# Attention inside a two-part transformer kernel: value products turned round, weights normalised on GpSimd before they are turned

## What is computed

```python
proj = u @ w_in
o_a = dsa_attention(aq, ak, av, iq, ik, iw)      # 4 heads, one shared key and value, the best 64 keys of each query
o_b = moba_attention(bq, bk, bv)                 # 4 heads, causal here (256 tokens are one block)
o_c = forgetting_attention(cq, ck, cv, log_f)    # 8 heads, score + cumsum(log_f)[query] - cumsum(log_f)[key]
o_c = o_c * jax.nn.sigmoid(cg)                   # a gate for each of the 512 output columns of o_c
return jnp.concatenate([o_a, o_b, o_c], axis=-1) @ w_out
```

## Time and profile before

| | |
|---|---|
| median of 3 runs | 2230.54 us (2229.44 to 2232.28) |
| the profiled execution | 2230.91 us, span 2229.2 us |
| PE busy | 2142.9 us, 96% of the span |
| DVE, ACT, POOL busy | 47%, 34%, 3% |
| attention turns of the first layer | 1438.9 to 1473.2 us in the span |
| attention turns of the second layer | 1973.8 to 2011.2 us in the span |

### The profile page before, as it was taken

One profiled execution on the slowest core, in us unless ns is written; L12 is line 12 of the kernel. 1 busy time (PEld: TensorE's weight loads), 2 busy tenths in 40 slices (PEclk: granted clock), 3 DMA queues, 4 the chain that ended last, 5 costly groups with the idle time before them and its releaser, 6 DMA issues.

```text
span 2229.2 us, 27344 instructions
## 1 busy us (share of the span) xinstructions
PE 2142.9 (96%) x10940; PEld 1422.5 (64%) x10940; DVE 1051.4 (47%) x1559; ACT 764.8 (34%) x1099; POOL 72.5 (3%) x100
## 2 busy tenths in 40 slices
PE   8999999988999999999889999999999999999999
PEld 6663333333486333333348888878888888888887
DVE  5830000001383000000147777768777777866776
ACT  4732111110272111111033436654335435565332
POOL 3000000000000000000100002000000000300000
PEclk9999999999999999999999999999999999999999
DMA  8389999999949999999985555235565554415551
GB/s 290 151 358 428 428 428 427 427 427 426 387 184 388 427 427 428 428 428 428 426 313 191 172 185 173 93 116 189 189 199 177 171 194 159 153 58 180 187 197 59
DMA packets 169816, 618.29 MB, mean 277 GB/s; under 512 B 7816, under 2 KB 116528, under 8 KB 145904
## 3 DMA queue, kind: packets, MB, share of 16 engines
q1 hardware_dynamic: 167248, 612.00, 70.8%
q0 software_dynamic: 2464, 4.84, 0.8%
HBM read 615.76 MB, written 1.05 MB: 277 GB/s over the span
## 4 chain that ended last, share of the span: by engine, by line
PE 76%; DMA 13%; DVE 4%; ACT 4%; SPq 1%; DVEq 1%; issue 1%; ACTq 0%
PE W L2172 20%; PE W L2419 12%; PE W L2420 6%; DMA moe_own<-in_moe_w 5%; DMA moe_split<-in_moe_w 4%; PE acc L2023 4%; PE acc L2027 4%; PE acc L2024 4%; PE W L1995 3%; PE W L1997 3%; PE W L1996 3%; PE W L2154 2%; DMA moe_raw<-in_moe_w 2%; DMA moe_xt<-in_moe_w 2%; PE W L2423 2%; PE acc L2163 2%
## 5 line engine op out<-in xcount | busy, mean ns | idle before, releaser
L1267 DVE TENSOR_TENSOR w_lo<-raw,w_hi 128x2048 fp32r<-128x2048 f32 (+2 forms) x203 | 445.0, 2195 | 168.9 <-ACT w_hi L771 160.4
L771 ACT ACTIVATE w_hi<-raw 128x2048 fp32r<-128x2048 f32 (+2 forms) x203 | 372.2, 1833 | 305.5 <-PE acc L2027 134.5
L2419 PE MATMUL W<-xT_both,w_hi 128*128 128x512 f32 x1218 | 438.1, 399 | 4.2 <-DVE xT_both L1285 3.4
L1543 DVE TENSOR_TENSOR hid<-W,hid 128x512 f32<-128x512 f32 x32 | 22.1, 691 | 732.2 <-PE W L2172 732.2
L2420 PE MATMUL W<-xT_both,w_lo 128*128 128x256 f32 x1218 | 341.7, 281 | 0.0
L2419 PEld LDWEIGHTS W<-xT_both,w_hi 128*128 128x128 f32 x1218 | 229.2, 188 | 55.4 <-issue 4.0
L2420 PEld LDWEIGHTS W<-xT_both,w_lo 128*128 128x128 f32 x1218 | 230.1, 189 | 7.0
L2172 PE MATMUL W<-moe_split,xe 128*64 128x512 f32 x672 | 150.5, 595 | 9.1 <-DMA moe_split<-in_moe_w 9.1
L2172 PE MATMUL W<-moe_own,xe 128*64 128x512 f32 x608 | 137.3, 596 | 12.5 <-DMA moe_own<-in_moe_w 12.4
L1995 PE MATMUL W<-w_hi,xT_both 128*128 128x474 f32 (+1 forms) x376 | 145.4, 387 | 0.0
L1996 PE MATMUL W<-w_lo,xT_both 128*128 128x474 f32 (+1 forms) x376 | 142.7, 380 | 0.0
(11 more groups left out here) (409 smaller groups left out, 2944.4 us busy)
## 6 DMA issues: line engine op xcount, KB each, us to landing
moe_split<-in_moe_w SPq DMA_DIRECT2D x60, 2048.0 KB, 29.9
moe_raw<-in_moe_w SPq DMA_DIRECT2D x54, 2048.0 KB, 31.8
moe_own<-in_moe_w SPq DMA_DIRECT2D x54, 2048.0 KB, 29.5
raw<-in_ffn_w_gate SPq DMA_DIRECT2D x44, 1024.0 KB, 5.1
raw<-in_ffn_w_up SPq DMA_DIRECT2D x44, 1024.0 KB, 5.1
raw<-in_ffn_w_down SPq DMA_DIRECT2D x44, 1024.0 KB, 4.8
moe_xt<-in_moe_w SPq DMA_DIRECT2D x18, 2048.0 KB, 34.0
raw<-in_w_in SPq DMA_DIRECT2D x32, 948.0 KB, 4.8
```

What stands on the lines that cost most here:

```text
L771: s.activation(part(w_hi[split_slot(c)], cols), part(raw[slot_of(c)], cols), ACT.Copy).then_inc(hi_ready, 1)
L1267: v.tensor_tensor(part(w_lo[split_slot(c)], cols), part(raw[slot_of(c)], cols), part(w_hi[split_slot(c)], cols).bitcast(F32), ALU.subtract ...
L2419: t.matmul(wide, hi[:, cols], xT_both[:, kc].rearrange("p h t -> p (h t)"), start=(kc == 0), stop=False)
```

## The change

- `finish` goes. DVE takes the reciprocal of the row sums right after the exponentials (`reciprocal_sums`), POOL multiplies the weights in place by it, four instructions a unit, and PE waits for POOL (`normal`) instead of ACT (`p`) before it turns the weights.
- The value product takes the 64 value columns of a head as the stationary matrix and streams 128 turned weights; two heads go to the two halves of the PSUM partitions. The result is already [head columns, tokens], so `turn_result` and `attn` go.
- The gates are turned once, after `decays`, and DVE copies them to `gate_T`. `apply_gate` multiplies the result in PSUM; `upper_result` on ACT and `lower_result` on DVE write the two halves that the output product reads.
- The forget sums of eight heads are packed into one product (four instructions for sixteen, a copy of 256 columns for 1024); `head_rows`, made by POOL, picks a head's row.
- `split` and `rest` of one chunk of `w_out` (c + 18) move from ahead of the first exponentials to behind unit 0's copy on ACT and behind `chosen_bias(0)` on DVE.

PE still waits for `at` of unit u-2 at the head of turn u. The semaphore is now raised by `lower_result`. The core of the diff:

```diff
@@ POOL, ahead of the turns and in them
                 g.memset(nlf_wide[:], 0.0)
+                g.tensor_tensor(head_rows[:], ident[:, 0:C_HEADS // 2].unsqueeze(2).to_broadcast([P, C_HEADS // 2, P]),
+                                ident[:, HD:HD + C_HEADS // 2].unsqueeze(2).to_broadcast([P, C_HEADS // 2, P]), ALU.add)
...
+                for u in range(8):
+                    n = P * (UNITS[u][0] + 1)
+                    pool.wait_ge(mx["recip"], 8 * l + u + 1)
+                    for i in range(4):
+                        last = g.tensor_scalar(Sb[:, u % 2, i, 0:n], Sb[:, u % 2, i, 0:n], asum[:, u, i:i + 1], None, ALU.mult)
+                    last.then_inc(mx["normal"], 1)
@@ ACT
-                split(c + 18, D)
...
+                def upper_result(u):
+                    b, grp = UNITS[u]
+                    if grp >= 2:
+                        act.wait_ge(mx["gated"], 4 * l + u - 1)
+                    else:
+                        act.wait_ge(mx["o"], (lay.times(8) + (u + 1)).v)
+                    s.activation(xT_hi[:, 2 * grp:2 * grp + 2, b * P:(b + 1) * P],
+                                 acc[:, 2 + u % 2, 0:SEQ].rearrange("p (a t) -> p a t", a=2), ACT.Copy).then_inc(mx["hi"], 1)
...
-                s.activation(decay_rows[:], acc[:, 0:2, :].rearrange("p a (i k) -> p (a i) k", k=SEQ), ACT.Copy).then_inc(mx["decay_sb"], 1)
+                s.activation(decay_rows[:], acc[:, 0, 0:SEQ], ACT.Copy).then_inc(mx["decay_sb"], 1)
                 for u in range(8):
...
-                    if u == 6:
-                        attention_halves(range(3))
+                    if u == 0:
+                        split(c + 18, D)
+                    else:
+                        upper_result(u - 1)
+                upper_result(7)
@@ DVE
+                def reciprocal_sums(u):
+                    dve.wait_ge(mx["p"], (lay.times(8) + (u + 1)).v)
+                    v.reciprocal(asum[:, u, :], asum[:, u, :]).then_inc(mx["recip"], 1)
+                def apply_gate(u):
                     b, grp = UNITS[u]
                     dve.wait_ge(mx["o"], (lay.times(8) + (u + 1)).v)
...
+                    v.tensor_tensor(result(u), result(u), gate_T[:, 2 * (grp - 2):2 * (grp - 1), b * P:(b + 1) * P], ALU.mult)
+                    v.drain().then_inc(mx["gated"], 1)
+                def lower_result(u):
+                    b, grp = UNITS[u]
+                    dve.wait_ge(mx["hi"], (lay.times(8) + (u + 1)).v)
+                    own = (slice(None), slice(2 * grp, 2 * grp + 2), slice(b * P, (b + 1) * P))
+                    v.tensor_tensor(xT_lo[own], result(u), xT_hi[own].bitcast(F32), ALU.subtract).then_inc(mx["at"], 1)
...
-                rest(c + 18, D)
                 maxima(0)
                 maxima(1)
+                dve.wait_ge(mx["gates"], l + 1)
+                v.tensor_copy(gate_T[:].rearrange("p k t -> p (k t)"), acc[:, 2:4, :].rearrange("p a n -> p (a n)"))
+                v.drain().then_inc(mx["gate_sb"], 1)
+                reciprocal_sums(0)
                 for u in range(8):
                     if u == 0:
                         best_keys(0, 4, 8)
                         chosen_bias(0)
+                        rest(c + 18, D)
                     elif u < 5:
                         best_keys(1, 2 * (u - 1), 2 * u)
                         if u == 4:
                             chosen_bias(1)
+                    if u < 7:
+                        reciprocal_sums(u + 1)
                     if u + 2 < 8:
                         maxima(u + 2)
...
-                    finish(u)
+                    if UNITS[u][1] >= 2:
+                        apply_gate(u)
+                    if u > 0:
+                        lower_result(u - 1)
+                lower_result(7)
@@ PE
+                    t.matmul(acc[:, 0, 0:SEQ], nlf_wide[:, 0, :], tri[:], start=True, stop=False)
+                    t.matmul(acc[:, 0, P:SEQ], nlf_wide[:, 1, :], tri[:, 0:P], start=False, stop=True).then_inc(mx["decay"], 1)
+                def turn_gates():
+                    for k in range(4):
+                        for b in range(TB):
+                            last = t.transpose(acc[:, 2 + k // 2, SEQ * (k % 2) + b * P:SEQ * (k % 2) + (b + 1) * P],
+                                               proj[:, b, CG + P * k:CG + P * (k + 1)], ident[:])
+                    last.then_inc(mx["gates"], 1)
...
+                turn_gates()
                 for u in range(8):
                     b, grp = UNITS[u]
                     if u == 0:
                         pe.wait_ge(mx["decay_sb"], l + 1)
+                        pe.wait_ge(mx["gate_sb"], l + 1)
                     if u >= 2:
 
                         pe.wait_ge(mx["at"], (lay.times(8) + (u - 1)).v)
                     if u < 6:
                         keep_warm(4, u)
-                    pe.wait_ge(mx["p"], (lay.times(8) + (u + 1)).v)
+                    pe.wait_ge(mx["normal"], (lay.times(8) + (u + 1)).v)
...
-                    if u == 6:
+                    if u == 7:
                         pe.wait_ge(mx["at"], (lay.times(8) + 6).v)
-                        pe.wait_ge(mx["p"], (lay.times(8) + 8).v)
-                        for q in TURN_ORDER[:3]:
-                            turn_result(q)
...
                     pe.wait_ge(mx["te"], (lay.times(8) + (u + 1)).v)
...
+                    for pair in range(2):
                         for kb in range(b + 1):
+                            for r in range(2):
+                                h = 2 * pair + r
+                                hh = 4 * (grp - 2) + h
+                                col = (AV, BV + HD * h, CV + HD * hh, CV + HD * hh)[grp]
+                                last = t.matmul(acc[HD * r:HD * (r + 1), 2 + u % 2, P * pair:P * (pair + 1)], proj[:, kb, col:col + HD],
+                                                PT[:, 2 * r + pair, kb * P:(kb + 1) * P], start=(kb == 0), stop=(kb == b))
                     last.then_inc(mx["o"], 1)
```

More of the change, by code:

```diff
@@ L325, in build_program @@
         place[0] = after_qkt
-        attn = at("attn", [P, TB, D])
+        gate_T = at("gate_T", [P, 4, SEQ])
         Sb = at("Sb", [P, 2, 4, SEQ])
@@ L348, in build_program @@
         score2 = in_proj("score2", 1, AQ, [P, SEQ])
-        decay_rows = in_proj("decay_rows", 0, CQ, [P, C_HEADS // 2, SEQ])
-        nlf_wide = in_proj("nlf_wide", 1, CQ, [P, TB, C_HEADS // 2, P])
+        decay_rows = in_proj("decay_rows", 0, CQ, [P, SEQ])
+        head_rows = in_proj("head_rows", 0, CQ + SEQ, [P, C_HEADS // 2, P])
+        nlf_wide = in_proj("nlf_wide", 1, CQ, [P, TB, P])
         acc = ctx.enter_context(nc.psum_tensor("acc", [P, 4, 512], F32))
@@ L1809, in chosen_bias, with result @@
                     v.drain().then_inc(mx["bias"], 1)
-                def finish(u):
+                def result(u):
+                    return acc[:, 2 + u % 2, 0:SEQ].rearrange("p (a t) -> p a t", a=2)
+                def reciprocal_sums(u):
+                    dve.wait_ge(mx["p"], (lay.times(8) + (u + 1)).v)
+                    v.reciprocal(asum[:, u, :], asum[:, u, :]).then_inc(mx["recip"], 1)
+                def apply_gate(u):
                     b, grp = UNITS[u]
                     dve.wait_ge(mx["o"], (lay.times(8) + (u + 1)).v)
[L1815 to L1826, removed]
+                    v.tensor_tensor(result(u), result(u), gate_T[:, 2 * (grp - 2):2 * (grp - 1), b * P:(b + 1) * P], ALU.mult)
[5 more added lines that the diff above has]
+                    v.tensor_tensor(xT_lo[own], result(u), xT_hi[own].bitcast(F32), ALU.subtract).then_inc(mx["at"], 1)
                 def maxima(u):
@@ L1914, in mixer @@
                             chosen_bias(1)
+                    if u < 7:
+                        reciprocal_sums(u + 1)
                     if u + 2 < 8:
                         maxima(u + 2)
-                    if u == 6:
-                        attention_rests(range(3))
-                    if u == 7:
-                        rest(c0 + (C_MIX_OUT + AHEAD), D)
-                    finish(u)
-                attention_rests((3,))
-                for k in range(1, KC - 2):
+                    if UNITS[u][1] >= 2:
[3 more added lines that the diff above has]
+                lower_result(7)
+                for k in range(0, KC - 2):
                     rest(c0 + (C_MIX_OUT + k + AHEAD), D if k + AHEAD < KC else SLOT)
@@ L2597, in scores @@
                             half = slice(HD * (h % 2), HD * (h % 2 + 1))
-                            t.matmul(W[:, k, o:o + n], tri[half, P:2 * P], decay_rows[half, hh // 2, 0:n], start=False, stop=False,
+                            t.matmul(W[:, k, o:o + n], head_rows[half, hh // 2, :], decay_rows[half, 0:n], start=False, stop=False,
                                      skip_group_check=True)
@@ L2633, in mixer @@
                         scores(u + 2)
[L2634 removed]
+                    if u == 7:
```

(5 more changed lines are left out.)

47 lines of the change are left out of this document (4 added, 43 removed).

## The result

The kernel after takes 2256.35 us (2254.43 to 2257.01), the one before 2230.39: a ratio of 1.0113 (95% interval 1.0101 to 1.0125), 26 us slower where 9.3 were forecast and 2252 was the top of the range. The profiled execution took 2257.01 us with a span of 2255.1. The whole difference lies in the two attention stretches: from the first scores to the first idle product behind the output chunks the first layer takes 77.69 us (1433.79 to 1511.48) where it took 64.02 (1433.44 to 1497.46), the second 79.12 where it took 67.25. That is 25.5 of the 26.

What follows compares the result with a forecast made beforehand. PE was taken as close to the bound, DVE behind it. Profiled execution 2230.91 + 6.1 for two layers' walk + 3.1 for the clock gave 2240.1, the median 0.4 lower at 2239.7 us; range 2230 to 2252.

Steps and rivals of the forecast that it cites:

- The mechanism forecast: Attention turns: PE waits for `at`, now raised behind maxima and gate on DVE; with about one more clock fall, chance 0.42.
- a wait of PE that ends on POOL: Sign in the profile after that would show the forecast wrong: PE's wait ending on POOL; no size given.
- The sum: Whole kernel: profiled execution 2230.91 + 6.1 for two layers + 3.1 for the clock = 2240.1 us, median 2239.7.
- so I take the first: POOL's multiplication ahead of the turnings, priced as one-input: 4 x 0.39 us for 256 keys, 4 x 0.29 for 128.
- the count of the clock's falls: Attention stretches: one fall of PE's clock in both layers instead of in one, +3.1 us.
- saves nothing there: Unit 2 to 3: PE idles about 2 us after the value product, so its shortening gains nothing; interval +1.8 us.
- The nearer wait: Head of PE's turn: `at` of unit u-2 comes one DVE turn later; unit 2 to 3 takes 6.05 instead of 4.27 us.
- POOL is the bound: Rival: POOL's multiplications at 0.953 us, four taking 3.8, add 6 us a layer: 2248.6 us; chance 0.08.
- those on the clock: Rivals: lower clock no oftener or never, 2236.6 or 2233.5 us, chance 0.27; low through most turns, 2245 to 2258, 0.10.
- the loop: Scores, maxima, gate and rest must follow one another before PE's next turn: 6.05 us from unit 2 to 3.
- Edits costed at nothing: `head_rows` on POOL, moved `split` and `rest`, ACT's short copies and POOL's queued loads: claimed hidden under waits or slack, 0 us.
- the late reciprocal: Unit 0 to 1: unit 1's reciprocal queues on DVE behind key search, mask and moved `rest`; interval +2.3 us.

Runs made afterwards that it cites:

- the mended kernel: After with POOL in one instruction, lower_result first, unit 1's reciprocal inside the key search, split and rest in units 5 and 6, some warming products: 2227.42 us.

## Why the prediction was right in direction and wrong in size

The mechanism forecast, PE held by `at` through DVE's queue, is in the trace, but it is not alone: PE also waits 5.7 us for POOL in the first layer and 8.8 in the second, and the prediction had named a wait of PE that ends on POOL as a sign that it was wrong. The sum was short by 17 us. The step that failed is "so I take the first", POOL's price: 0.39 us was taken and 0.93 measured. With it failed the count of the clock's falls: one a layer was taken, and there were three and four. The intervals of the first layer, in us between starts of turnings:

| interval | before | predicted | measured | what makes the difference |
|---|---|---|---|---|
| first scores to unit 0 | 7.73 | 7.4 | 8.94 | POOL 2.35 instead of 1.16; selector 0.4 |
| unit 0 to 1 | 3.43 | 5.7 | 7.81 | POOL 3.63 instead of 1.56; unit 0's delay carried on through `split` and `rest` |
| unit 1 to 2 | 4.76 | 4.58 | 6.71 | half clock |
| unit 2 to 3 | 4.27 | 6.05 | 6.05 | none |
| unit 3 to 5 | 10.22 | 11.2 | 12.46 | clock at unit 4 |
| unit 5 to first chunk | 9.41 | 9.05 | 11.76 | POOL 3.63 instead of 1.66; half clock at unit 7's turning (0.6) |
| chunks | 24.20 | 23.1 | 23.96 | half clock at their start |

- *Value products.* 1.07 and 0.54 were priced; the rows show 1.09 and 0.66 with the pipeline's tail. The edit does what it says. That it "saves nothing there" fits the idle time behind it; doubling the products did not lengthen the kernel (2250.45), though the clock rose with it.
- *The nearer wait.* 6.05 predicted, 6.05 measured; with the lower half first, 4.15. What is left without POOL's excess and the clock's is 5.3 us over before (6.6 with before's own gap filled), against 6.1 in the sum.
- *POOL.* Priced from a one-input row at 0.39, with 4 x 0.95 named as the far end; measured 926 ns, so at the far end. The row chosen was a different operation (an affine select) that shared only the number of tensors. The rival "POOL is the bound" had this price and 0.08. Reduced to 1.04 and 1.90 us, 10.7 us go; without it, 17.1; both hold a part of the clock's loss. The Trainium skill, page GPSIMD Engine Reference, section Engine selection, has GpSimd near line rate for one input; here one input with a number per partition cost 926 ns for 256 columns, so the measurement decides against that half of its rule for this instruction.
- *Clock.* One fall a layer was counted, for the forecast's gaps of about 2 us. POOL's waits came on top, and there were three in the first layer and four in the second. Filling the gaps gave back 8.7 us. The two mistakes are one: the longer wait also made PE slow behind it, and no rival had both: the one on POOL's price (2248.6) was summed without any added fall, those on the clock with POOL's low price. No case held POOL's price, the loop and the clock together, which is what came, so the range ended at 2252. The Trainium skill, page TensorE: Matmul & The Clock Gate, section What's actually happening, says "the default state is throttled, and activity releases the throttle"; the runs agree, since idle products and doubled ones raised the granted clock and shortened the time.
- *Edits costed at nothing.* The selector was not free: 0.4 us a layer at the start. The moved `rest` cost more than its 1.23: DVE stood 1.50 us ahead of it for the `split`, which sits behind unit 0's copy, and that copy had become late by POOL. Moved behind, both were part of the mended kernel; no run moved them alone. The moved loads and ACT's short copies cost nothing that the trace shows.

The parts add up: POOL near its predicted price and the clock filled take 20.6 of the 26.0 us away (10.7 and 8.7 singly), and the 5.3 left fit the loop, the late reciprocal and the start, of which only the loop's order (3.7 in after) and the start (0.9, below what the times tell) were changed by themselves.

## What to carry to other kernels

Price a new instruction from a row of the same operation with the same kinds of operands; where there is none, sum the case at the far end of the price with everything that a longer wait brings along, the clock too, before the range is closed. Making the busiest engine's work shorter saves nothing where another queue sets its turns, and the idle time it leaves can cost more than the work did. Where a signal moves to the end of another engine's queue, look first whether the instruction that raises it can stand ahead of the long one: here that, one POOL instruction in place of four, an earlier reciprocal, and `split`, `rest` and the selector moved back brought a loss of 26 us to nothing. The filled waits then brought a gain of 4 to 5 over before; before, too, gains 1.6 when its own gap is filled, and beside the clock no gain is shown.

## What the runs showed of the hardware

- On POOL the multiplication by one number a partition (926 ns for 256 columns, 605 for 128, so 2.5 ns a column) is dearer than the two-tensor multiplication whose second input is a broadcast of the same numbers (1895 ns for 1024 columns, 1041 for 512, so 1.7 ns a column; with a plain second tensor 953 for 256): 3.63 us against 1.90 for the same work. The price was the same with POOL's step put into before (927 ns), where DVE's queue has another order.
- Two heads beside each other in halves of 64 columns take 1.09 us for sixteen products of 128 columns, where the old form took 1.89 for sixteen of 64.
- In before the same gap of 1.45 us had no fall of the clock behind it in one layer and one in the other, and less work ahead of a wait (the packed forget sums) was enough to bring a fall where there had been none.
